# Two transformer blocks on one core: x comes turned from the host, and its norm's root moves behind the matmuls

## What is computed

```python
h = rms_norm(x, g_mix)                 # x / sqrt(mean(x*x) + 1e-6) * g_mix
p = h @ w_in                           # 8,272 columns: a, qm, gq, ck, gk, gv, r, q, gates
m = rms_norm(mem, g_mem) @ w_mem_kv    # keys and values of the memory
```

## Time and profile before

| | us |
|---|---|
| three runs | 928.07, 5160.74, 927.0 |
| median of the runs | 928.07 |
| profiled execution | 928.21 |
| its span, first to last instruction | 926.6 |
| TensorE busy | 905.8 |
| VectorE busy | 720.2 |
| ScalarE busy | 534.9 |

### The profile page before, as it was taken

The page is one execution under the profiler, slowest core; times in us unless marked ns, Lnnn a source line. Parts: engine busy times, 40 slices in busy tenths (PEclk is TensorE's granted clock), DMA queues, the critical chain, the costliest instruction groups (busy, mean ns, idle before and its releaser), DMA issues.

```text
span 926.6 us, 13743 instructions
## 1 busy us (share of the span) xinstructions
PE 905.8 (98%) x4668; PEld 731.7 (79%) x4668; DVE 720.2 (78%) x1030; ACT 534.9 (58%) x831; POOL 162.7 (18%) x247
## 2 busy tenths in 40 slices
PE   8999999999999999999999999999999999999996
PEld 7888888777878778888888887666678688888885
DVE  4779476878778778887679788865668879999976
ACT  6775754476766565555333345655674676666633
POOL 8000000216600000110112001650000023444400
PEclk9999999999999999999999999999999999999999
DMA  8856844876653447887598755322245465555572
GB/s 317 204 150 203 275 137 127 282 268 198 182 180 105 142 142 251 270 268 251 174 351 306 249 159 185 122 73 77 92 138 179 150 193 178 171 174 177 173 251 78
DMA packets 100534, 176.16 MB, mean 190 GB/s; under 512 B 8560, under 2 KB 36592, under 8 KB 100352
## 3 DMA queue, kind: packets, MB, share of 16 engines
q1 hardware_dynamic: 93120, 149.87, 50.8%
q0 software_dynamic: 7184, 25.50, 8.3%
q10 hardware_dynamic: 176, 0.08, 0.0%
HBM read 174.38 MB, written 1.05 MB: 189 GB/s over the span
## 4 chain that ended last, share of the span: by engine, by line
PE 57%; DVE 5%; ACT 2%; issue 1%; DMA 1%; DVEq 0%
PE acc L775 49%; PE turned L1257 2%; PE scores L1246 1%; PE turned L867 1%; DVE wlo L1944 1%; PE turned L1359 1%; PE turned L1146 1%; PE turned L1169 1%; PE turned L811 1%; DMA raw<-in_w_out 1%; ACT prob L1796 0%; ACT whi L1399 0%; DVE soft L2649 0%; DVE turn L2031 0%; PE turned L1261 0%
## 5 line engine op out<-in xcount | busy, mean ns | idle before, releaser
L1944 DVE TENSOR_TENSOR wlo<-raw,whi 128x1024 fp32r<-128x1024 f32 (+3 forms) x269 | 346.1, 1306 | 83.2 <-ACT whi L1399 72.6
L1399 ACT CAST whi<-raw 128x1024 fp32r<-128x1024 f32 (+3 forms) x269 | 273.3, 1032 | 161.2 <-PE acc L775 114.5
L775 PE MATMUL acc<-whi,lta_hi 128*128 128x512 f32 (+2 forms) x576 | 163.4, 399 | 0.2 <-DVEq L2521 0.2
L775 PE MATMUL acc<-whi,lta_lo 128*128 128x512 f32 (+2 forms) x576 | 155.8, 385 | 0.0
L775 PE MATMUL acc<-wlo,lta_hi 128*128 128x512 f32 (+2 forms) x576 | 155.4, 385 | 0.0
L775 PEld LDWEIGHTS acc<-whi,lta_hi 128*128 128x128 f32 x576 | 101.2, 188 | 30.6 <-issue 10.5
L775 PEld LDWEIGHTS acc<-whi,lta_lo 128*128 128x128 f32 x576 | 106.9, 188 | 22.3
L775 PEld LDWEIGHTS acc<-wlo,lta_hi 128*128 128x128 f32 x576 | 106.9, 188 | 21.9
L657 POOL DMA_DIRECT2D wm<-in_w_mod x48 | 34.5, 721 | 427.6 <-DVEq L2075 244.6
L775 PE MATMUL acc<-whi,ltb_hi 128*128 128x512 f32 (+1 forms) x268 | 73.2, 391 | 1.1 <-ACT ltb_hi L1857 0.8
L775 PE MATMUL acc<-wlo,ltb_hi 128*128 128x512 f32 (+1 forms) x268 | 71.2, 384 | 1.6 <-DVE wlo L1944 1.6
(11 more groups left out here) (371 smaller groups left out, 1304.5 us busy)
## 6 DMA issues: line engine op xcount, KB each, us to landing
raw<-in_w_in SPq DMA_DIRECT2D x88, 512.0 KB, 4.4
wm<-in_w_mod POOLq DMA_DIRECT2D x48, 512.0 KB, 6.1
raw<-in_w_up SPq DMA_DIRECT2D x88, 256.0 KB, 3.1
raw<-in_w_up SPq DMA_DIRECT2D x32, 512.0 KB, 4.6
raw<-in_w_down SPq DMA_DIRECT2D x32, 512.0 KB, 5.5
raw<-in_w_down SPq DMA_DIRECT2D x44, 256.0 KB, 3.3
raw<-in_w_o SPq DMA_DIRECT2D x8, 512.0 KB, 4.6
raw<-in_w_out SPq DMA_DIRECT2D x8, 512.0 KB, 4.0
```

Of the source, the lines that this page charges most:

```text
L775: ins = pe.matmul(acc[s][:, t, 0:n], lhs[part][:, kt0 + kk, tok], w[:, u % RING, kk, 0:n], start=(opens and k == 0 and kk == 0 and j == 0) ...
L1399: act.copy(whi[:, s, :, 0:n], raw[:, s, :, 0:n]).then_inc(hi_ready, 1)
L1944: dve.tensor_tensor(wlo[:, s, :, 0:n], raw[:, s, :, 0:n], whi[:, s, :, 0:n].bitcast(F32), ALU.subtract)\
```

## The change

The host lays out x turned as well (`x_t`), and AQ's 272 columns as one contiguous array (`w_aq`), and puts the eight small gain vectors into one array. SP loads the turned x in four pieces behind the units of MK2, the memory's token rows behind MK2's second and third unit, and x's token rows behind GQ's first two units; the convolution's columns, the first layer norm's columns and the positions follow AQ and not MK2. ScalarE and VectorE scale the turned x with g_mix straight from memory into `lta`, without the root. TensorE turns nothing. The root is taken behind MK2's evacuation and multiplied in wherever a panel of h leaves PSUM: the evacuations become one instruction for each token tile, with the root as scale (`normed_rows`), r's sigmoid and its product too, and the gates' bias addition becomes a multiply and add for each token tile. The copy of the very first weight tile moves from ScalarE to VectorE, and ScalarE's first instruction is a square root, so that its table is loaded then.

```diff
-    out += [("AQ", KT, 2)]
+    out += [("AQ", KT, 1)]
...
-                return [(0, rows(w, k)[:, :, COL["a"]:COL["a"] + GATE_RANK]),
-                        (GATE_RANK, rows(w, k)[:, :, COL["qm"]:COL["qm"] + 256])]
+                return [(0, a["w_aq"][:, UNIT * k:UNIT * k + UNIT, :])]
...
-                    if name == "MK1" and k == units_of(name) - 1:
-                        for t in range(T):
+                    if name == "MK2":
+                        sp.dma_start(xT[:, 2 * k:2 * k + 2, :], a["x_t"][:, 2 * k:2 * k + 2, :])\
+                          .then_inc(ev(f"xT{k}_landed"), 16)
+                        if k in (1, 2):
+                            t = k - 1
                             sp.dma_start(memx[:, t], a["mem"][t * P:(t + 1) * P, :]).then_inc(ev(f"mem{t}_landed"), 16)
-                    if name == "MK2" and k < T:
+                    if name == "GQ" and k < T:
                         sp.dma_start(x[:, k], a["x"][k * P:(k + 1) * P, :]).then_inc(ev(f"x{k}_landed"), 16)
...
-            for name, view in GAIN.items():
-                pool.dma_start(view, a[name].partition_broadcast(P)).then_inc(ev("gains_landed"), 16)
+            pool.dma_start(gains[:], a["gains"].partition_broadcast(P)).then_inc(ev("gains_landed"), 16)
...
-            for k in range(4):
-                if k == 3:
-                    pe.wait_ge(ev("h_scaled"), T)
-                    turn_tokens("h", work, groups=(0, 1))
-                unit("MK2", k, ltb)
-            turn_tokens("h", work, groups=(2, 3))
+            panel("MK2", ltb)
             panel("AQ", lta, NARROW["AQ"], new="h")
...
-                    act.wait_ge(ev("first_landed"), 16)
-                    act.copy(whi[:, 0, 0], raw[:, 0, 0]).then_inc(ev("first_hi"), 1)
...
-            act.activation(stat[:, 0, 8:9], ident[:, 0:1], ACT.Copy, scale=ident[:, 1:2])
+            act.activation(stat[:, 0, 8:9], ident[:, 0:1], ACT.Sqrt)
...
+            for g in range(4):
+                ahead(2 + g)
+                if g >= 2:
+                    row_squares("mem", memx, 0, g - 2)
+                lt_act("h", lta, (g,))
+            sqrt("mem", stat[:, 0, 2:4])
...
             normed_memory("MK1", kvm[:, :, 256:768], COLS)
-            ahead(PLAN.unit["MK2"] + 2)
-            lt_act("h", lta, (0, 1))
-            ahead(PLAN.unit["MK2"] + 3)
-            lt_act("h", lta, (2, 3))
             normed_memory("MK2", kvm[:, :, 768:1280], COLS)
-            evac("AQ", aq[:], NARROW["AQ"])
+            for t in range(T):
+                ahead(last_unit("AQ") + t)
+                row_squares("x", x, 1, t)
+            sqrt("x", stat[:, 1, 2:4])
...
+                for t in range(T):
+                    ins = act.activation(dst[:, t], acc[s][:, t, 0:n], ACT.Copy, scale=stat[:, 1, 2 + t:3 + t])
+                ins.then_inc(panel_out[s], 1)
+
+            normed_rows("AQ", aq, NARROW["AQ"])
...
-            for t in range(T):
-                dve.tensor_scalar(work[:, t], x[:, t], stat[:, 1, 2 + t:3 + t], None, ALU.mult)\
-                   .then_inc(ev("h_scaled"), 1)
...
+            ahead(last_unit("AQ"))
+            row_var("x", 1)
+            inverse("x", stat[:, 1, 2:4])
+            dve.sem_inc(ev("x_inverse"), 1)
             ahead(PLAN.unit["GQ"])
             evacuated("AQ")
+            dve.wait_ge(ev("conv_columns_landed"), 32)
...
-                    frees(name, dve.tensor_tensor(v, p[:], rsig, ALU.mult))
+                    for t in range(T):
+                        ins = dve.scalar_tensor_tensor(v[:, t], p[:, t], stat[:, 1, 2 + t:3 + t], rsig[:, t], ALU.mult, ALU.mult)
+                    frees(name, ins)
...
-                dve.tensor_tensor(p[:], p[:], bias[:, n % 2].unsqueeze(1).broadcast_to([P, T, COLS]), ALU.add)\
-                   .then_inc(gate_in, 1)
+                for t in range(T):
+                    ins = dve.scalar_tensor_tensor(p[:, t], p[:, t], stat[:, 1, 2 + t:3 + t], bias[:, n % 2],
+                                                   ALU.mult, ALU.add)
+                ins.then_inc(gate_in, 1)
```

More of the change, by code:

```diff
@@ L171, in t_names @@
     mod = lambda first, n: [f"{v}.{c}" for c in range(first, first + n) for v in ("mod", "modt")]
-    out = g("h", 4) + ["aT", "z.0", "z.1", "mqT", "mkT", "ck"]
+    out = ["aT", "z.0", "z.1", "mqT", "mkT", "ck"]
     out += attention_t("MEM", H_MEM)
@@ L289, in hybrid_kernel @@
         ln_sums = sb("ln_sums", [P, T, 8])
-        gains = sb("gains", [P, 6 * 64 + DV_GLA + HEADS])
+        gains = sb("gains", [P, sum(n for _, n in GAINS)])
         ROWS, at = {}, 0
@@ L584, in _ @@
                     panel(name)
-                if name == "MK2":
+                if name == "AQ":
                     sp.dma_start(ccol[:], a["columns"][:, 96:96 + 8 * FT2].rearrange("p (v r) -> p v r", v=4))\
@@ L1424, in lt_act @@
                     if name in LT_DIRECT:
-                        if name == "me":
-                            act.wait_ge(ev(f"memT{g}_landed"), 16)
+                        if name in LT_HOST:
+                            act.wait_ge(ev(f"{'memT' if name == 'me' else 'xT'}{g}_landed"), 16)
                         else:
@@ L1515, in _, with row_squares @@
                 ahead(g - 2)
-            for name, src, s in (("me", memx, 0), ("h", x[:], 1)):
-                for t in range(T):
[L1519 to L1525, removed]
+            def row_squares(name, src, s, t):
+                act.wait_ge(ev(f"{name}{t}_landed"), 16)
+                act.activation(prob[:].rearrange("p a b -> p (a b)"), src[:, t, :], ACT.Square,
+                               accum_out=stat[:, s, t:t + 1]).then_inc(ev(f"{name}_sum"), 1)
+                act.wait_ge(ev(f"{name}_sum"), t + 1)
+            for g in range(4):
[4 more added lines that the diff above has]
+            sqrt("mem", stat[:, 0, 2:4])
             def normed_memory(name, dst, n):
@@ L2167, in _, with row_var @@
             dve.wait_ge(ev("columns_landed"), 16)
+            dve.wait_ge(ev("first_landed"), 16)
+            dve.tensor_copy(whi[:, 0, 0], raw[:, 0, 0]).then_inc(ev("first_hi"), 1)
             lt_dve("me", ltb, col("g_mem", 0, 8), between=lambda g: ahead(g - 2), sent=memT)
-            for name, s in (("me", 0), ("h", 1)):
-                ahead(2 + 2 * s)
+            def row_var(name, s):
                 dve.wait_ge(ev(f"{name}_sum"), T)
@@ L2173, in _ @@
                     .then_inc(ev(f"{name}_var"), 1)
[L2174 to L2178, removed]
-                dve.tensor_scalar(work[:, t], x[:, t], stat[:, 1, 2 + t:3 + t], None, ALU.mult)\
-                   .then_inc(ev("h_scaled"), 1)
-            ahead(PLAN.unit["MK2"] + 1)
-            dve.wait_ge(ev("conv_columns_landed"), 32)
-            ahead(PLAN.unit["MK2"] + 2)
-            lt_dve("h", lta, col("g_mix", 0, 8), groups=(0, 1))
-            ahead(PLAN.unit["MK2"] + 3)
-            lt_dve("h", lta, col("g_mix", 0, 8), groups=(2, 3))
-            ahead(PLAN.unit["AQ"])
+            for g in range(4):
+                ahead(2 + g)
+                lt_dve("h", lta, col("g_mix", 0, 8), groups=(g,))
+            row_var("mem", 0)
+            inverse("mem", stat[:, 0, 2:4])
+            dve.sem_inc(ev("mem_inverse"), 1)
+            ahead(last_unit("AQ"))
+            row_var("x", 1)
+            inverse("x", stat[:, 1, 2:4])
+            dve.sem_inc(ev("x_inverse"), 1)
             ahead(PLAN.unit["GQ"])
             evacuated("AQ")
+            dve.wait_ge(ev("conv_columns_landed"), 32)
             views = []
@@ L2907, in laid_out @@
         + [in_columns(inputs[name]) for name in ("conv_b_2", "ln1_g_2", "ln1_b_2")], axis=1))
-    arrays["in_mem_t"], arrays["in_ctx_t"] = turned_tokens(inputs["mem"]), turned_tokens(inputs["ctx_2"])
+    for name in ("x", "mem"):
+        arrays[f"in_{name}_t"] = turned_tokens(inputs[name])
+    arrays["in_ctx_t"] = turned_tokens(inputs["ctx_2"])
     return arrays
```

55 lines of the change are left out of this document (33 added, 22 removed).

## The result

The changed kernel takes 929.42 us (median of 11 runs, 928.73 to 930.76) against 927.77 us before; the ratio is 1.0021 with a 95% interval of 1.0014 to 1.0029. Two of the eleven runs before, 5160.74 and 3468.08 us, are left out of the ratio, and the median of the other nine is 927.29 us. That is no change by the 2% bound, but a small loss that the runs resolve. The profiled execution has a span of 927.8 us, 1.2 more than before, at 929.42 us.

A forecast was written before the change was run, and what follows sets the result against it. TensorE, busy 98% of the span, bounds the kernel; a 3.5 us lead at AQ, less 1.0 + 0.95 + 0.7 + 1.2, becomes 0.4 late: 928.21 + 0.4 = 928.6, said as 928.5 us against the median. Range 924.9 to 931.0.

The forecast's parts named there:

- AQ's start: After MK2: AQ begins near 31.5 us, not 30.5, behind ScalarE's chain and cast; 1.0 of the 3.5 lead is lost.
- The gain of the first copy: At the opening: first matmul near 6.6 or 6.7 us, not 6.95; 0.2 us taken, at least 0, at most 0.4.
- The loads: GQ's weights: u12 lands at 36.4 us, then x0, u13, x1, u14 at 1.32 each, u14 at 41.7.
- rival B: GQ's loads: the burst through u14 does not keep 397 GB/s; at 300 four transfers take 1.7 more, 930.2 us; chance 0.20.
- The root and the three stops: GQ and CK: root at 44.7 us, then the angles, make TensorE wait 0.95, 0.7 and 1.2 for VectorE's splits.
- From the gate on nothing regains or loses a lead: Behind the decay gate: VectorE's start and TensorE's next long chain begin from the same matmuls, so no lead changes.
- I take 0 of the 3.6: Doubled instructions for the root: 2.4 us on evacuations and sigmoids, 1.2 on VectorE, all taken as hidden.
- Waits past 100 us that the kernel before did not have: Late in the kernel: new TensorE waits there were named as a sign that the prediction is wrong.
- a panel's bank has 11 us to come free: Evacuations carrying the root: a bank has a whole panel of 11 us, so none delays a cast TensorE waits for.
- Rival C: Doubled instructions show in full on TensorE: 928.5 + 3.6 = 932.1 us; chance 0.06.
- It brings nothing: AQ panel: one contiguous load a unit instead of two gains nothing, as ScalarE casts that unit late anyhow.

The follow-up runs named there:

- the last experiment: Early load of x's rows and other VectorE/ScalarE order, plus ScalarE casting AQ's first two units ahead of the memory's root, against the kernel before: 925.31 us, ratio 0.9981.
- the four experiments with the same loads: Changed kernel without x's root (928.04 us), with another VectorE/ScalarE order (927.67), with VectorE's doubled instructions single again (928.69), with ScalarE's single again (929.57).
- the two with instructions undone: Changed kernel with VectorE's doubled instructions as one again, 928.69 us (1.0019), and with ScalarE's as one again, 929.57 us (1.0025).
- the first four experiments: Changed kernel without x's root (928.04 us), with x's rows loaded earlier (927.66), with another VectorE/ScalarE order (927.67), with the last two together (927.25).
- the kernel with both edits: Changed kernel with x's rows loaded early behind AQ's third and fourth unit and another order of VectorE and ScalarE: 927.25 us, ratio 0.9999 to the kernel before.

## Why the prediction was right, and where it was not

The class was right, the sign of the change too, and 929.42 us lies in the range; the point, 928.5, was 0.9 short. Most of the working holds, but a term set at zero was not zero, and two numbers of its middle are right partly by luck.

**AQ's start.** Forecast 31.5, measured 31.09. The reason given, ScalarE's chain ahead of the first AQ cast, is confirmed by the last experiment, which moves that cast and removes the wait. GQ's first matmul, forecast 37.6, came at 37.18 with it.

**The gain of the first copy.** Forecast 0.2. The first matmul is at 6.91, so 0.04 in this execution; in six of the seven experiments that open with VectorE's copy it is at 6.62 to 6.76, as forecast. It is worth nothing here either way, since AQ waits for ScalarE's cast.

**The loads.** GQ's third unit was to land at 41.7; its cast began at 41.66. That the two agree is luck:

```profile
35.67 1.05 ACT L1393 CAST whi<-raw 128x1024 fp32r<-128x1024 f32 x1 [1.93 <-DMA raw<-in_w_in]
...
41.66 1.05 ACT L1393 CAST whi<-raw 128x1024 fp32r<-128x1024 f32 x1 [0.68 <-ACT prob L1514]
```

The squares named in the second row were done at 40.99; the cast waited for its load. The first unit, forecast for 36.4, was there at 35.67, and the four transfers behind it took 5.99 us, 1.50 each or 350 GB/s, where the sum had 1.32 and 397. In the four experiments with the same loads they took 6.02 to 6.32. So rival B's mechanism is real, in the changed kernel at under half its price (0.7 us more and not 1.7). What hangs on it shows between executions: in the changed kernel and the two with instructions undone the third cast began at 41.66, 42.27 and 42.33 and the gate at 55.32, 55.91 and 55.98. The Trainium skill (DMA: Bandwidth & Descriptors, "Where 436 GB/s comes from") says that HBM binds such loads at about 358 GB/s, by which one would take an estimated 1.46 us. The landings are nearer to that than to 1.32, but as a bound it does not hold here: from 38.88 to 41.66 us the queues moved 399 GB/s.

**The root and the three stops.** Root forecast for 44.7, its reciprocal ended at 44.46; the split's end at 45.9, measured 45.84. Stops of 0.95, 0.7 and 1.2 were forecast, 1.17, 0.74 and 0.87 came. Their sum was right (2.85 against 2.78); left out was the slower restart behind each, and with it and small stops GQ to gate lost 3.39. The gate came at 55.32, forecast 55.2. That the gate is so near is luck in part, since AQ's 0.41 of more lead and this 0.54 of more loss all but cancel. As the cause I named the root, then the angles behind it. The runs show the root as about half: without it 1.46 of the loss stays, most of it the third stop, which is the angles' place in VectorE's order and does not need a late root. With x's loads early 1.57 stays, with another order but the late loads 1.44, with both cured 0.05.

**"From the gate on nothing regains or loses a lead" and "I take 0 of the 3.6".** This is the step that failed: 0.57 us are lost there, 0.54 of them to VectorE's doubled instructions. Waits past 100 us that the kernel before did not have were a sign of being wrong; what came are waits that it had, made longer, 0.61 to 0.78 near 207 us and 0.15 to 0.34 near 312. The argument was that a panel's bank has 11 us to come free. That holds for the bank, but three of the bias additions stand on VectorE ahead of work for which TensorE waits soon after. ScalarE's share of the 3.6 was rightly taken as hidden. Rival C was the right mechanism at a sixth of its price.

**"It brings nothing" for the AQ panel.** For the changed kernel no run tests the step: AQ's start was worked out from ScalarE's order, and came so. What I missed is that part of the gain was to be had without the rest of the change, since the panel alone is worth 1.19 us at AQ in the kernel before. I had read the name in the wait (VectorE) and not followed it back through ScalarE's order to the landing.

The rest of the 1.2 us between the two spans is 0.15 near 710 us, where the weights of the output projection land late by an amount that differs from one execution to the next. ScalarE's last cast of them waits 2.50 us for the landing before and 2.9 after, and VectorE's work on x, for which TensorE waits, stands behind the split of that tile:

```profile
722.40 1.11 PE L1332 MATMUL turned<-ident,x_res 128*128 128x128 f32 x8 [0.47 <-DVE x_res L2776]
```

```profile
723.59 0.66 PE L1328 MATMUL turned<-ident,x_res 128*128 128x128 f32 x4 [0.62 <-DVE x_res L2790]
```

That wait is 0.47 before, 0.62 after, and 0.20 to 1.27 in the first four experiments, so I take it as scatter and no part of the change. The medians are 1.65 us apart, 2.13 by the 927.29 of the nine runs, and the profiled executions 1.21. The profiled execution before took 928.21, more than any of the nine, and the forecast's starting point, 928.07, stood 0.8 above their median; what made that execution longer no trace shows.

## What to carry to other kernels

Work taken from the bounding engine is worth only what the next thing in time allows: here 2.9 us of lead met weights that could not be split sooner, because unrelated small work (a root, the angles) stood ahead of the splits in a fixed order. Do that small work where its engine waits for loads, put feeding instructions ahead of it, and load what a chain needs in a stretch where the queues are idle. And follow a named wait back engine by engine: a stop put down to VectorE was a late landing, and instructions split in two for a scale cost their extra time wherever the other engine waits for what stands behind them.

## What the runs showed of the hardware

Narrow loads took more of the queues' time than their bytes say. From 22 to 34 us the kernel before had 1,733 of 3,310 packets below 512 bytes (the 16 columns of AQ are rows of 64 bytes); with the one array it had 649 of 2,303, moved more bytes in the same time (2.33 MB against 2.17), and the first AQ cast began 1.35 us earlier. SP's queue took 61.8% of the engines' time for 1.85 MB before, and 57.7% for 2.04 MB with the one array.

The opening differs between executions of the same instructions. In the changed kernel the first matmul began at 6.91 and two of them took 1.19 us; in the kernel with both edits, which opens alike, they began at 6.67 and took 0.70. The granted clock shows 1.00 (the 2.4 GHz level) in both. MK2's last unit began at 27.98 in the one and 26.85 in the other. What decides this was not tried.

TensorE's clock fell behind an idle stretch in one execution, and the gate was hardly later for it. With VectorE's instructions undone TensorE stood idle for 1.93 us before AQ, and from 31.5 to 35.1 us the granted clock was 0.54, near the lower level of 1.2 GHz. AQ took 7.66 us and not 6.09, and GQ began at 39.23, 2.05 us later than in the changed kernel. The gate began only 0.59 later, as late as GQ's third cast was: the splits, not TensorE, set it. With x's rows loaded earlier TensorE stood idle for 2.01 us there, and AQ took 6.09 all the same; why the clock fell in the one and not in the other was not tried.
